# Raw chunks rounded amid the residual's tiles, feed-forward output tiles interleaved by bank, and a mixing norm spread by transpositions

## The reference

```python
def rms_norm(x, g):
    y = x * rsqrt(mean(x * x, axis=-1) + 1e-6)
    return y * g
# 512 tokens, D = 1024; two layers of first_block, then second_block
for l in range(2):
    x = x + 0.5 * swiglu_ffn(rms_norm(x, g_ffn1[l]), w_up1[l], w_down1[l])      # 1024 -> 2 x 2816 -> 1024
    h = rms_norm(x, g_mix[l]); z = h @ w_in[l]
    # a recurrent branch (conv, gated scan) and a 16-head attention branch from z
    x = x + (gate_lru * y_lru + gate_attn * y_attn) @ w_o[l]
    x = x + 0.5 * swiglu_ffn(rms_norm(x, g_ffn2[l]), w_up2[l], w_down2[l])
# second_block (one layer): rmsnorm -> w_in -> conv + sparse attention -> w_out, residual;
# attention over a memory, w_mem_o, residual; rmsnorm -> PEER experts, residual; final rmsnorm
```

## Time and profile before

| | |
|---|---|
| median of 3 runs | 4690.24 us |
| the profiled execution | 4695.69 us |
| its span, first to last instruction | 4693.7 us |
| TensorE busy | 4488.5 us (96%) |
| weight loads of TensorE busy | 3758.4 us (80%) |
| VectorE / ScalarE / GpSimd busy | 2743.5 / 1738.7 / 615.8 us |
| mean granted TensorE clock | 0.979 of full |

### The profile page before, as it was taken

The page is one execution under the profiler, slowest core; times in us unless marked ns, Lnnn a source line. Parts: engine busy times, 40 slices in busy tenths (PEclk is TensorE's granted clock), DMA queues, the critical chain, the costliest instruction groups (busy, mean ns, idle before and its releaser), DMA issues.

```text
span 4693.7 us, 61860 instructions
## 1 busy us (share of the span) xinstructions
PE 4488.5 (96%) x22059; PEld 3758.4 (80%) x22059; DVE 2743.5 (58%) x4451; ACT 1738.7 (37%) x2861; POOL 615.8 (13%) x639
## 2 busy tenths in 40 slices
PE   8999999999999999999999989899899899999998
PEld 6887788878878887788878878687666788888887
DVE  5436545454434436555454268754796877777777
ACT  3224524332222325344332232343225744444444
POOL 0000000000000000000000000000385622222221
PEclk9999999999999999999999997999999999999999
DMA  3222220122222222211222222022223588888887
GB/s 125 97 99 90 81 72 36 64 89 98 99 87 102 98 90 81 90 54 36 90 90 98 99 74 90 1 91 77 75 81 115 224 311 299 293 308 295 293 310 255
DMA packets 86659, 605.07 MB, mean 129 GB/s; under 512 B 10752, under 2 KB 11136, under 8 KB 19904
## 3 DMA queue, kind: packets, MB, share of 16 engines
q1 hardware_dynamic: 58320, 412.95, 24.3%
q0 software_dynamic: 27136, 162.28, 10.2%
q10 hardware_dynamic: 1008, 27.26, 1.4%
HBM read 573.09 MB, written 29.36 MB: 128 GB/s over the span
## 4 chain that ended last, share of the span: by engine, by line
PE 85%; DVE 6%; ACT 3%; issue 2%; DVEq 2%; ACTq 1%; DMA 1%; SPq 0%; POOL 0%; POOLq 0%
PE PB L189 24%; PE PB L191 24%; PE PB L190 24%; PE PB L2554 3%; PE PB L905 2%; PE PB L1129 2%; PE PB L2805 1%; PE PB L895 1%; PE PB L2821 1%; ACT WH L2961 1%; PE PB L1142 1%; PE PB L2069 1%; DVE PT L945 0%; DVE XL L238 0%; DVE WL L3011 0%
## 5 line engine op out<-in xcount | busy, mean ns | idle before, releaser
L189 PE MATMUL PB<-XH,WH 128*128 128x512 f32 (+1 forms) x3280 | 1258.1, 384 | 62.2 <-DVE WL L170 23.6
L190 PE MATMUL PB<-XL,WH 128*128 128x512 f32 (+1 forms) x3280 | 1245.6, 380 | 0.0
L191 PE MATMUL PB<-XH,WL 128*128 128x512 f32 (+1 forms) x3280 | 1245.5, 380 | 0.0
L170 DVE TENSOR_TENSOR WL<-RAW,WH 128x1024 fp32r<-128x1024 f32 x520 | 642.3, 1274 | 509.9 <-ACT WH L162 490.5
L189 PEld LDWEIGHTS PB<-XH,WH 128*128 128x128 f32 x3280 | 622.3, 190 | 174.8 <-issue 25.1
L162 ACT ACTIVATE WH<-RAW 128x1024 fp32r<-128x1024 f32 x506 | 507.8, 1049 | 556.9 <-PE PB L191 533.6
L190 PEld LDWEIGHTS PB<-XL,WH 128*128 128x128 f32 x3280 | 622.5, 190 | 103.4 <-issue 1.4
L191 PEld LDWEIGHTS PB<-XH,WL 128*128 128x128 f32 x3280 | 621.6, 190 | 101.6
L248 POOL TENSOR_TENSOR SQ<-SQ 128x512 f32<-128x512 f32 x49 | 70.3, 1435 | 2666.9 <-ACT SQ L231 2657.0
L3011 DVE TENSOR_TENSOR WL<-RAW,WH 128x1024 fp32r<-128x1024 f32 x220 | 269.6, 1225 | 221.2 <-ACT WH L2961 221.1
L189 PE MATMUL PB<-WH,WGH 128*128 128x512 f32 x768 | 301.1, 392 | 12.4 <-DVE WGL L3027 12.4
(11 more groups left out here) (407 smaller groups left out, 7313.1 us busy)
## 6 DMA issues: line engine op xcount, KB each, us to landing
RAW<-weights SPq DMA_DIRECT2D x382, 1024.0 KB, 4.8
gate_matrix<-STG ACTq DMA_DIRECT2D x6, 4096.0 KB, 12.3
GM<-gate_matrix POOLq DMA_DIRECT2D x128, 192.0 KB, 4.0
RAW<-weights SPq DMA_DIRECT2D x10, 512.0 KB, 3.9
X<-x SPq DMA_DIRECT2D x4, 512.0 KB, 5.5
x_home<-X ACTq DMA_DIRECT2D x1, 2048.0 KB, 6.3
UV<-rows,IDX POOLq DMA_INDIRECT x128, 6.0
AE<-x_home SPq DMA_DIRECT2D x1, 2048.0 KB, 13.8
```

Source lines behind the costliest of these rows:

```text
L170: c.nc.vector.tensor_tensor(c.WL[p][:, cols], c.RAW[p][:, cols], c.WH[p][:, cols].bitcast(F32), ALU.subtract).then_inc(c.sem("w_split"), 1)
L189: c.nc.tensor.matmul(out, wh, xh, start=start, stop=False)
L190: c.nc.tensor.matmul(out, wh, xl, start=False, stop=False)
L191: return c.nc.tensor.matmul(out, wl, xh, start=False, stop=stop)
```

## The change

1. *Residual.* `act_residual` takes a callback `raw`: behind each weight split from the second on, it rounds and squares the two chunks of the tile before. This goes for both w_o residuals and for w_mem_o; `act_raw` behind them goes. On VectorE the low parts stand ahead of the wait for the next tile, no longer behind its addition.
2. *Feed-forward.* A chunk order `DOWN_ORDER = (0, 1, 6, 7, 2, 3, 4, 5)`. The last but one down tile does six banks only; its parts for banks 4 and 5 come in the midst of the last tile, behind the first four banks. So the last tile and its insert have 60 matmuls and the one before 36. ScalarE's raw chunks and VectorE's additions stand half ahead of the next tile's weight split (`DOWN_EARLY`), half behind it (`DOWN_LATE`). The raw chunks of the next layer's first norm (and of the second block's) stand here too, ahead of the layer loop's branch, with a new gain column `g_next` in the parameters.
3. *Mixing head.* TensorE starts when four chunks are new (banks 0, 1, 6, 7), takes chunks in `DOWN_ORDER`, waits for all eight and the sum of squares behind its fifth chunk, and sums per token only (bank 5). The root and the reciprocal are of 128x4; VectorE copies them out to 128x512 (RB), and TensorE turns RB into bank 4 by four transpositions behind its seventh chunk. `dve_chase` reads bank 4 in place of RB. The weight split amid it comes two chunks later on both engines.
4. *Start.* X is loaded in pairs 0, 6, 2, 4, and the first raw chunks stand ahead of the loop.

The diff, cut to its core:

```diff
+DOWN_ORDER = (0, 1, 6, 7, 2, 3, 4, 5)
...
@@ act_chase
-    for k in range(DC):
-        act.wait_ge(c.sem("nx_ready"), w * DC + (k + 1))
-        free(k)
+    for i, k in enumerate(order):
+        act.wait_ge(c.sem("nx_ready"), w * DC + (i + 1))
+        free(i)
         c.nc.scalar.activation(c.XH[:, k, :], N.SQ[:, k, :], ACT.Copy).then_inc(c.sem("nx_hi"), 1)
-        if k == 3 and between:
+        if i == 5 and between:
             between()
@@ dve_chase
-    for k in range(DC):
-        V.scalar_tensor_tensor(out=N.SQ[:, k, :], in0=c.X[:, k, :], scalar=g(k), in1=N.RB[:, :],
+    for i, k in enumerate(order):
+        V.scalar_tensor_tensor(out=N.SQ[:, k, :], in0=c.X[:, k, :], scalar=g(k), in1=c.PB[:, 4, :],
                                op0=ALU.mult, op1=ALU.mult).then_inc(c.sem("nx_ready"), 1)
...
-        if k == 4 and between:
+        if i == 6 and between:
             between()
@@ pe_raw_tokens
-    pe.wait_ge(c.sem("x_new"), x_stage(v) * DC + DC)
+    pe.wait_ge(c.sem("x_new"), x_stage(v) * DC + len(banks))
...
-        last.then_inc(c.sem("chunk_used" if k < DC - 1 else "tile_done"), 1)
-        if k == 2:
-            pe_sum(c, pe, v, N, tokens=True)
+        last.then_inc(c.sem("chunk_used" if i < DC - 1 else "tile_done"), 1)
+        if i == 4:
+            pe.wait_ge(c.sem("x_new"), x_stage(v) * DC + DC)
+            pe.wait_ge(c.sem("sq_sum"), v + 1)
+            for tb in range(QB):
+                last = c.nc.tensor.matmul(c.PB[:, 5, tb:tb + 1], N.SQ[:, 0, tb * P:tb * P + P], c.ONES[:, 0:1],
+                                          start=True, stop=True)
+            last.then_inc(c.sem("norm_sum"), 1)
+        if i == 6:
+            pe.wait_ge(c.sem("norm_wide"), w + 1)
+            for tb in range(QB):
+                last = c.nc.tensor.transpose(c.PB[:, 4, tb * P:tb * P + P], N.RB[:, tb * P:tb * P + P], c.IDENT[:, :])
+            last.then_inc(c.sem("norm_spread"), 1)
@@ dve_mix_head
-    dve_scale(c, dve, v, N, tokens=True)
-    dve_chase(c, dve, w, N, g, lambda: dve_next(c, dve, Tile(cur, 0, 0, 1)))
+    dve.wait_ge(c.sem("norm_root"), v + 1)
+    c.nc.vector.reciprocal(c.RT[:, :], c.RT[:, :]).then_inc(c.sem("tok_ready"), 1)
+    dve.drain()
+    c.nc.vector.tensor_copy(N.RB[:, :].rearrange("p (t d) -> p t d", t=QB),
+                            c.RT[:, :].unsqueeze(2).to_broadcast([P, QB, P])).then_inc(c.sem("norm_wide"), 1)
+    dve.wait_ge(c.sem("norm_spread"), w + 1)
+    dve_chase(c, dve, w, N, g, lambda: dve_next(c, dve, Tile(cur, 0, 0, 1)), DOWN_ORDER)
@@ pe_ffn
+        if k0 == FC // 2 - 2:
+            for kk in range(2):
+                pe_half(c, pe, tile.t, kk)
+                for m in DOWN_ORDER[:6]:
+                    part(tile, m, kk, False, False)
+            before = tile
+            continue
         if k0 == FC // 2 - 1:
             pe_half(c, pe, tile.t, 1)
-            for m in range(DC):
-                part(m, 0)
-                part(m, 1).then_inc(c.sem("x_part" if m < DC - 1 else "tile_done"), 1)
+            for i, m in enumerate(DOWN_ORDER):
+                if i == 4:
+                    for rest in DOWN_ORDER[6:]:
+                        for kk in range(2):
+                            last = part(before, rest, kk, False, False)
+                    last.then_inc(c.sem("tile_done"), 1)
+                part(tile, m, 0, False, False)
+                part(tile, m, 1, False, True).then_inc(c.sem("x_part" if i < DC - 1 else "tile_done"), 1)
@@ act_ffn
     for tile, k0 in down_tiles(act, cur):
+        if k0 == FC // 2 - 1:
+            raw(DOWN_EARLY)
         act_next(c, act, tile)
...
+    raw(DOWN_LATE)
+DOWN_EARLY, DOWN_LATE = range(4), range(4, DC)
@@ dve_ffn
     for tile, k0 in down_tiles(dve, cur):
+        if k0 == FC // 2 - 1:
+            for i in DOWN_EARLY:
+                add(tile, i)
+                if i:
+                    low((i - 1,))
         dve_next(c, dve, tile)
...
+    for i in DOWN_LATE:
+        low((i - 1,))
+        add(tile, i)
+    low((DC - 1,))
@@ act_residual
     for j in range(4):
         act_next(c, act, one_tile(cur))
+        if raw and j:
+            raw((j * 2 - 2, j * 2 - 1))
...
+    if raw:
+        raw((DC - 2, DC - 1))
@@ dve_residual
         dve_next(c, dve, tile)
+        if low and j:
+            low((j * 2 - 2, j * 2 - 1))
         dve.wait_ge(c.sem("tile_done"), tile.t + 3)
...
-        if low and j:
-            low((j * 2 - 2, j * 2 - 1))
```

More of the change, by code:

```diff
@@ L316, in pe_first_tile @@
     WL = c.WL[tile.p][:, :].rearrange("p (k m c) -> p k m c", k=DC, m=2)
[L317 to L319 removed]
+    upper = order.index(max(order[:DC // 2 + 1], key=lambda k: k >= DC // 2))
+    for i, k in enumerate(order):
+        pe.wait_ge(c.sem(lo), base + (i + 1))
+        if i == upper:
             pe_half(c, pe, tile.t, 1)
@@ L429, in pe_ffn @@
                         pe.wait_ge(c.sem("silu"), f * FC + FC)
-                last = part(m, kk)
+                last = part(tile, m, kk, k0 == 0 and kk == 0, False)
         last.then_inc(c.sem("tile_done"), 1)
@@ L484, in dve_ffn, with add @@
                         ALU.subtract).then_inc(c.sem("h_lo"), 1)
-    for tile, k0 in down_tiles(dve, cur):
+    def add(tile, i):
+        if i < DC - 1:
+            dve.wait_ge(c.sem("x_part"), f * (DC - 1) + (i + 1))
+        else:
+            dve.wait_ge(c.sem("tile_done"), tile.t + 3)
+        xs = c.X[:, DOWN_ORDER[i], :]
+        V.scalar_tensor_tensor(out=xs, in0=c.PB[:, DOWN_ORDER[i], :], scalar=0.5, in1=xs,
+                               op0=ALU.mult, op1=ALU.add).then_inc(c.sem("x_new"), 1)
+    for tile, k0 in down_tiles(dve, cur):
+        if k0 == FC // 2 - 1:
+            for i in DOWN_EARLY:
+                add(tile, i)
+                if i:
+                    low((i - 1,))
         dve_next(c, dve, tile)
@@ L488, in dve_ffn @@
             first_down()
-    for m in range(DC):
-        if m < DC - 1:
-            dve.wait_ge(c.sem("x_part"), f * (DC - 1) + (m + 1))
-        else:
-            dve.wait_ge(c.sem("tile_done"), tile.t + 3)
-        xs = c.X[:, m, :]
-        V.scalar_tensor_tensor(out=xs, in0=c.PB[:, m, :], scalar=0.5, in1=xs,
-                               op0=ALU.mult, op1=ALU.add).then_inc(c.sem("x_new"), 1)
-        if low and m:
-            low((m - 1,))
-    if low:
-        low((DC - 1,))
+    for i in DOWN_LATE:
+        low((i - 1,))
+        add(tile, i)
+    low((DC - 1,))
 def wax_pairs(cur):
```

152 lines of the change are left out of this document (79 added, 73 removed).

## The result

The changed kernel took 4670.41 us in the median of 7 runs (4658.03 to 4679.40); the kernel before, run beside it, 4690.93 (7 runs, 4689.13 to 4696.36). The ratio is 0.9947, 95% interval 0.9936 to 0.9958. It is faster, as forecast, but by 20.5 us between the medians (24.9 by the ratio) and not by 36.6: the forecast of 4653.6 is a ratio of 0.9922, and the median lies above the range's upper end of 4665. Two later comparisons, on two other groups of runs, gave ratios of 0.9944 and 0.9938.

The account below looks back on a forecast made before the run. TensorE, busy 96% of the span, bounds the kernel; only its stops and lower clock matter. Savings of 26.5 + 0.3 + 6.3 + 3.5 = 36.6 us from 4690.24 gave 4653.6 us, range 4646 to 4665.

Parts of the forecast that it names:

- term C: Mixing head, three times: TensorE starts earlier, with a new 2.0 us stop; 0.8, 0.8 and 1.85, together 3.5 us go.
- term B: Layer loop, layer 0 to 1: raw chunks ahead of the branch remove the stop and slow matmuls; 6.3 us go.
- Residual, 26.5 + 0.3 us: Both w_o residuals and w_mem_o: stops and slow stretches go, 26.5 us; shorter sum-of-squares wait ahead of PEER, 0.3 us.
- The stop "doesn't go": Rival at the residual: something else, a late weight load or the rounding, ends the stop; time 4680, chance 0.03.
- the rival of a chain longer than a tile: Residuals: split, raw chunks, low parts and addition exceed a 10.87 us tile, stopping each tile; time 4735, chance 0.03.
- TensorE's branch: Layer loop: queued matmuls cover it, costing nothing; rival: array runs dry for 3.78 us, time 4659.7, chance 0.13.
- 0.6 us back: Layer loop: after a 2.75 us branch the next weight split ends at T0 + 12.6, wanted at 12.0, losing 0.6 us.
- the late chain: Additions behind the split run serially: addition, rounding, low part, next addition, 2.35 us a chunk; 2.0 us mixing-head stop.
- the sign against C: Mixing head: head lengths above 32 us would prove the forecast saving there wrong.
- the mixing head gains nothing: Rival: serial late chunks and the 2.0 us stop cost what the start gives; -0.8 us, time 4658, chance 0.15.

## Why the prediction was half right

The forecast fell outside its range by two steps. One is the premise that everything outside the edited places stays as in the one profile, with a scatter of 2 to 3 us: in the profiled pair the light stages took 14.8 us more, and this is the larger part. The other is term C, the mixing head, which gave 1.8 us or a loss instead of 3.5, together with term B, 4.5 to 4.8 us instead of 6.3.

**Residual, 26.5 + 0.3 us.** Right. The two w_o stages gave 9.25 and 9.07 us in all three profiles. From the second w_mem_o tile to the first product of PEER it takes 32.65 us instead of 40.88, 8.2 less. The wait for the sum ahead of PEER fell from 2.25 to 1.70, 0.55 where 0.3 was taken. The stop "doesn't go" and the rival of a chain longer than a tile are out: ScalarE needs 4.28 us of the tile's 10.87.

**TensorE's branch.** Right against its rival: covered. It took the sequencer 3.56 us, to its next instruction at 1359.3, and the array went on 0.1 us behind T0. On ScalarE, which had no work queued there, 1.80 us of idle issue stand at the branch (loop timeline above). The rule of the Trainium skill ("Runtime: NRT & Kernel Launch", instruction fetch mechanics), that a taken branch to a target outside the fetched window stalls until that is fetched, agrees with the gap on ScalarE; the trace does not show what fills it.

**Layer loop, 6.3 us.** Mis-sized: 4.5, 4.8 and 4.8 in the three profiles. The stop that I had priced at "0.6 us back" measured 1.86 in the first. The last late addition started at T0 + 6.4 where I had 5.7, and between ScalarE's last square and the split stood the idle 1.80 us and a table load of 1.28, 3.1 together, where I had 2.75. The Trainium skill ("ScalarE: Activation LUTs", what ACT_TABLE_LOAD costs) gives about 1.28 us for the load itself; the rows agree. I had used VectorE's branch for ScalarE's, and VectorE has no table to load.

**Mixing head, 3.5 us.** The term that failed worst. Most pieces were right: the late chain's cadence of 2.35 us to the hundredth, the later stops of 0.89 and 2.15 us; the copy took 0.43 us where 0.69 was taken. But the chain began 0.5 us later, since the split ahead of it takes 2.85 us beside GpSimd instead of 2.36 and has a low part behind it. The stop became 2.6 us, and the head 32.1 us, not 31.5, with one slow stretch. In the second profile all three heads had a second or third one (35.2, 33.6 and 33.6 us), in the third profile two had (33.6). That is above the 32 us that the prediction named as the sign against C. Set against the first profile of the kernel before, term C came to 1.8, -4.4 and -1.3 us; that kernel's own heads scatter too, 33.5 for 32.3 us in layer 0 in its second profile. The rival "the mixing head gains nothing", at 0.15, had the place right, and its bound of -0.8 was too mild. The prediction priced the serial chain, but did not ask what the order of the kernel before would give in its place.

**What no term held.** The sum put everything else at nothing, with "an execution's scatter of 2 to 3 us". The 19 runs of the changed kernel lie between 4658.03 and 4683.52. In the first pair of profiles this is the light stages' clock: of the 16.7 us that the pair falls short of 36.6, it took 14.8.

That the rest came within 2 us of the forecast is in part luck. The terms as found add up to 33.3, 27.4 and 30.6 us in the three profiles, beside 34.7, 33.3 and 35.0 in the rest. The other 1.4 to 5.9 us came from places that no term held.

The median over all runs of the changed kernel is 4667.20, of the kernel before 4696.62 (97 runs). This is 29.4 us, beside 33 to 35 in the rest; by the difference the light stages are 4 to 6 us longer on average. Why, is open: no run separates the edited stages ahead of them from what changes between executions. A last point is the base. The three runs at hand had 4690.24, and the kernel's later medians lie 4 to 7 us above it, two of them above the profiled execution that I had called 5.45 too long. This doesn't explain the first comparison, where the kernel before had 4690.93.

## What to carry over

Before summing what an edit saves, see which stretches of the profile run between the two levels of TensorE's clock. Where they hold much of the span (here 18%), take a second profile of the unchanged kernel before giving a range; judge a part by the time outside them, and only then by the median. When a late value feeds two engines in turn, issue the next producer ahead of the hand-back: a few lines moved here, in a loop over four chunks, were worth 13 to 17 us, and without them the new mixing head gave nothing that repeats.

## What was unexpected of the hardware

- The same instructions in the light stages took 840.5 to 866.0 us. Attention of a layer took 270.3 us at a granted clock of 1.00 and up to 279.9 at 0.96; the compression stage 296.7 at 0.93 and 314.1 at 0.86. The Trainium skill ("TensorE: Matmul & The Clock Gate", part on the HAM clock gate) says that the activity is judged in windows that run free of the program, which would scatter just so; the runs show the scatter, not its cause.
- With 9.1 us of products added, one program fell into two groups of times, 4692 to 4697 and 4713 to 4720 us, with nothing between. What chooses the group is not shown.
- Filling a stop of 2.6 us with unused products shortened a head by 1.4 us or more, and the clock stayed at 2.4 GHz behind it.
- A weight split on VectorE of 2.36 us took 2.85 us (changed kernel) to 3.43 us (pipelined) in the mixing heads, beside GpSimd's additions.

The best version measured is the changed kernel with the late chain pipelined: 4651.75 and 4649.26 us on two occasions, 0.9898 of the kernel before (0.9884 to 0.9913 in the wider of both intervals), against 0.9938 to 0.9947 for the change as it was given.
